# The opening of a two-layer decoder trunk: x, constants, first slabs and first squares in another order

## The reference

```python
for l in range(DEPTH):
    h = rms_norm(x, norm_mix[l])
    q, k, v, hq, hf, hi, hg, cb, cc, ch = split(h @ w_in[l])
    a = sliding window attention with sinks (q, k, v and the cached keys and values)
    o = HGRN2 linear attention (hq, hf, hi, hg), chunked, with a lower bound on the gate
    yc = short convolution of cc * ch
    x = x + concat([a, o, cb * yc]) @ w_out[l]
    h = rms_norm(x, norm_ffn[l])
    gate, up = split(h @ w_gate_up[l])
    x = x + (silu(gate) * up) @ w_down[l]
y = rms_norm(x, norm_final)
```

## Time and profile before

| what | value |
|---|---|
| median of 3 runs | 2764.82 us (2761.4 to 2767.15) |
| span of the profiled execution, first to last instruction | 2763.7 us |
| TensorE busy | 2700.1 us, 98% |
| VectorE busy | 1529.2 us, 55% |
| ScalarE busy | 994.3 us, 36% |
| GpSimd busy | 359.0 us, 13% |
| mean granted clock of TensorE | 0.981 of full |

### The profile page before, as it was taken

The page is one execution under the profiler, slowest core; times in us unless marked ns, Lnnn a source line. Parts: engine busy times, 40 slices in busy tenths (PEclk is TensorE's granted clock), DMA queues, the critical chain, the costliest instruction groups (busy, mean ns, idle before and its releaser), DMA issues.

```text
span 2763.7 us, 53927 instructions
## 1 busy us (share of the span) xinstructions
PE 2700.1 (98%) x19968; PEld 2643.5 (96%) x19968; DVE 1529.2 (55%) x2163; ACT 994.3 (36%) x1322; POOL 359.0 (13%) x343
## 2 busy tenths in 40 slices
PE   6999999999999999999999999999999999999997
PEld 6998899999999999999999898999999999999997
DVE  6465757755554445454544566676555544555555
ACT  3343244433333333333333333344333333333332
POOL 3010101311110001111100011112111100111111
PEclk9999999999999999999999999999999999999998
DMA  6432333454545545444444232335445454454543
GB/s 235 160 116 100 118 123 118 146 173 153 173 161 168 166 152 168 166 160 167 156 164 153 100 131 99 129 125 169 165 157 176 153 175 160 156 169 160 167 169 125
DMA packets 115430, 420.09 MB, mean 152 GB/s; under 512 B 13072, under 2 KB 14352, under 8 KB 115280
## 3 DMA queue, kind: packets, MB, share of 16 engines
q1 hardware_dynamic: 109152, 397.72, 43.1%
q0 software_dynamic: 3168, 14.04, 1.5%
q10 hardware_dynamic: 3024, 7.16, 0.7%
HBM read 411.06 MB, written 11.87 MB: 153 GB/s over the span
## 4 chain that ended last, share of the span: by engine, by line
PE 91%; DVE 4%; issue 2%; ACT 1%; DMA 1%; ACTq 0%; DVEq 0%; POOL 0%; POOLq 0%
PE gp L1343 29%; PE gp L1345 28%; PE gp L1344 27%; PE mb L1396 2%; DVE wlo L628 1%; DVE qp L799 1%; PE mb L1446 1%; PE mb L1412 1%; PE mb L1479 1%; DVE xl L1043 1%; PE mb L1534 0%; PE mb L1491 0%; PE mb L1451 0%; DMA x<-x_in 0%; ACT whi L382 0%
## 5 line engine op out<-in xcount | busy, mean ns | idle before, releaser
L1343 PE MATMUL gp<-xh,whi 128*128 128x288 f32 x4096 | 1239.4, 303 | 29.8 <-DVE wlo L628 27.3
L1344 PE MATMUL gp<-xl,whi 128*128 128x288 f32 x4096 | 1219.2, 298 | 0.0
L1345 PE MATMUL gp<-xh,wlo 128*128 128x288 f32 x4096 | 1215.5, 297 | 0.0
L628 DVE TENSOR_TENSOR wlo<-raw,whi 128x1024 fp32r<-128x1024 f32 x754 | 971.4, 1322 | 369.8 <-ACT whi L382 366.1
L382 ACT ACTIVATE whi<-raw 128x1024 fp32r<-128x1024 f32 x754 | 769.6, 1052 | 622.1 <-PE gp L1345 608.8
L1343 PEld LDWEIGHTS gp<-xh,whi 128*128 128x128 f32 x4096 | 778.7, 190 | 41.8 <-DVE wlo L628 29.3
L1345 PEld LDWEIGHTS gp<-xh,wlo 128*128 128x128 f32 x4096 | 781.6, 191 | 0.0
L1344 PEld LDWEIGHTS gp<-xl,whi 128*128 128x128 f32 x4096 | 780.0, 190 | 1.3
L1343 PE MATMUL gp<-fh,whi 128*128 128x288 f32 x1408 | 416.7, 296 | 0.0
L1344 PE MATMUL gp<-fl,whi 128*128 128x288 f32 x1408 | 415.4, 295 | 0.0
L1345 PE MATMUL gp<-fh,wlo 128*128 128x288 f32 x1408 | 414.0, 294 | 0.0
(11 more groups left out here) (239 smaller groups left out, 2105.0 us busy)
## 6 DMA issues: line engine op xcount, KB each, us to landing
raw<-wstream SPq DMA_DIRECT2D x754, 512.0 KB, 4.0
s<-s_cache POOLq DMA_DIRECT2D x8, 512.0 KB, 4.0
hs_out<-s ACTq DMA_DIRECT2D x8, 512.0 KB, 2.6
caches_out<-caches POOLq DMA_DIRECT2D x1, 3968.0 KB, 15.6
x<-x_in ACTq DMA_DIRECT2D x4, 576.0 KB, 10.4
y_out<-x SPq DMA_DIRECT2D x4, 576.0 KB, 2.8
kct<-kt_cache POOLq DMA_DIRECT2D x4, 512.0 KB, 3.5
vct<-v_cache POOLq DMA_DIRECT2D x4, 512.0 KB, 5.0
```

The source lines that it names most:

```text
L628: v.tensor_tensor(wlo[slot][:], raw[slot][:], whi[slot][:].bitcast(F32), ALU.subtract).then_inc(lo_ready, 1)
L1343: t.matmul(out, w_hi, mv_hi, start=first, stop=False)
L1344: t.matmul(out, w_hi, mv_lo, start=False, stop=False)
L1345: mm = t.matmul(out, w_lo, mv_hi, start=False, stop=last)
```

## The change

Only the order of work changes; what is computed stays the same.

- GpSimd asks for the constants when all four quarters of x have landed. (The copy of the caches stays behind the adds.)
- ScalarE does a one-column copy first, then the exponential of the lower bound, and then, four times, the high part of one slab (0 to 3) and of one quarter of x. VectorE follows in the same order: wlo of a slab, then xl of a quarter.
- The first squares move to ScalarE, behind the last quarter of x, into two buffers in turn (`sq2`, `gs`). GpSimd only adds them. A square from the third on waits for the add before the last.
- The hi and lo of slabs 2 and 3 are out of the first group, and ScalarE's squares take their places between the hi of slabs 4 and on. The first root and its reciprocal come behind the second group, and TensorE does the mean-square products after slab 6 instead of after slab 3.
- So that layer 0 can differ from layer 1, the loop over layers is written out on ScalarE, VectorE, GpSimd and TensorE. TensorE's program has 6186 rows in place of 3241, VectorE's 1192 for 835, ScalarE's 857 for 562, GpSimd's 183 for 166.

```diff
--- before.py
+++ after.py
@@ -273,6 +273,8 @@
         xh_new = sem("xh_new")
         xl_new = sem("xl_new")
         sq_new = sem("square_steps")
+        sq_first = sem("first_squares")
+        sq_added = sem("first_squares_added")
         ms_ready = sem("mean_square_ready")
         root_ready = sem("root_ready")
         rstd_ready = sem("rstd_ready")
@@ -522,11 +524,12 @@
                 a.activation(out[:, 4:8, SEQ:TOK], asb[:], ACT.Copy).then_inc(aa.sem, aa.step("sah"))
                 yield
 
-            def group(n4, s0, m, fills=()):
+            def group(n4, s0, m, fills=(), ready=LEAD):
 
 
                 for s in range(m):
-                    hi(n4, s0 + s + LEAD)
+                    if s + LEAD >= ready:
+                        hi(n4, s0 + s + LEAD)
                     for fill in fills:
                         next(fill, None)
 
@@ -549,23 +552,38 @@
                     pair(i)
 
             a.wait_ge(ones_set, 4)
+            a.activation(one_col[:, 1:2], eps[:], ACT.Copy)
             a.wait_ge(par_loaded, 16)
-            hi(0, 0)
+            a.wait_ge(lb_steps, 2 * DEPTH)
+            a.activation(lbt[:, 2, :], lbt[:, 1, :], ACT.Exp).then_inc(lb_exp, 1)
             for j in range(KC // 2):
+                if j % 2 == 0:
+                    hi(0, j // 2)
                 a.wait_ge(x_loaded[j // 2], 16)
                 for c in range(2 * j, 2 * j + 2):
                     m = a.activation(xh[:, c, :], x[:, c, :], ACT.Copy, scale=par[:, P_AT[P_GAIN] + c:P_AT[P_GAIN] + c + 1])
                 m.then_inc(xh_new, 1)
-                if j == 3:
-                    hi(0, 1)
-            a.wait_ge(lb_steps, 2 * DEPTH)
-            a.activation(lbt[:, 2, :], lbt[:, 1, :], ACT.Exp).then_inc(lb_exp, 1)
-            with a.Fori(0, DEPTH) as l:
+
+            def first_squares():
+
+                for j in range(KC // 2):
+                    if j > 1:
+                        a.wait_ge(sq_added, j - 1)
+                    a.activation((sq2, gs)[j % 2][:], x[:, 2 * j:2 * j + 2, :], ACT.Square).then_inc(sq_first, 1)
+                    if j % 2:
+                        yield
+            for l in range(DEPTH):
                 n4 = l * (SLABS // RING)
                 g = l * GROUPS
-                group(n4, 0, 4)
-                root(l * 2)
-                group(n4, 4, 4)
+                if l == 0:
+                    fill = first_squares()
+                    group(n4, 0, 4, (fill,), ready=4)
+                    group(n4, 4, 4, (fill,))
+                    root(0)
+                else:
+                    group(n4, 0, 4)
+                    root(l * 2)
+                    group(n4, 4, 4)
                 with a.Fori(1, 4) as i:
                     group(n4 + i * 2, 0, 8)
                 a.wait_ge(group_out, hgrn_in(l))
@@ -628,9 +646,10 @@
                 v.tensor_tensor(wlo[slot][:], raw[slot][:], whi[slot][:].bitcast(F32), ALU.subtract
                                 ).then_inc(lo_ready, 1)
 
-            def group(n4, s0, m, fills=()):
+            def group(n4, s0, m, fills=(), ready=LEAD):
                 for s in range(m):
-                    lo(n4, s0 + s + LEAD)
+                    if s + LEAD >= ready:
+                        lo(n4, s0 + s + LEAD)
                     for fill in fills:
                         next(fill, None)
 
@@ -1037,16 +1056,14 @@
             for l in range(DEPTH):
                 lb_step(v.tensor_tensor(lbt[:, 1, l * nh:(l + 1) * nh], lb_col(l), top, ALU.subtract))
             for j in range(KC // 2):
+                if j % 2 == 0:
+                    lo(0, j // 2)
                 v.wait_ge(x_loaded[j // 2], 16)
                 v.wait_ge(xh_new, j + 1)
                 for c in range(2 * j, 2 * j + 2):
                     m = v.scalar_tensor_tensor(xl[:, c, :], x[:, c, :], par[:, P_AT[P_GAIN] + c:P_AT[P_GAIN] + c + 1],
                                                xh[:, c, :].bitcast(F32), ALU.mult, ALU.subtract)
                 m.then_inc(xl_new, 1)
-                if j == 1:
-                    lo(0, 0)
-                if j == 3:
-                    lo(0, 1)
             v.wait_ge(lb_exp, 1)
             lb_step(v.tensor_copy(lbt[:, 0, 0:nh], lbt[:, 2, 0:nh]))
             for l in range(1, DEPTH):
@@ -1061,7 +1078,7 @@
                 lb_step(v.tensor_scalar(oml[:, l * nh:(l + 1) * nh], cur, -1.0, 1.0, ALU.mult, ALU.add))
                 lb_step(v.tensor_scalar(lbc[:, l * nh:(l + 1) * nh], cur, LB_TINY, None, ALU.max))
 
-            with v.Fori(0, DEPTH) as l:
+            for l in range(DEPTH):
                 n4 = l * (SLABS // RING)
                 g = l * GROUPS
                 def in_groups(i):
@@ -1072,7 +1089,15 @@
                         used(n4 + i * 2, 4 * b + 4)
                         out_proj(b, 4 * i + 2 * b)
 
-                in_groups(0)
+                if l == 0:
+                    group(n4, 0, 4, ready=4)
+                    group(n4, 4, 4)
+                    finish_rstd(0)
+                    for b in range(2):
+                        used(n4, 4 * b + 4)
+                        out_proj(b, 2 * b)
+                else:
+                    in_groups(0)
                 with v.Fori(1, 4) as i:
                     in_groups(i)
                 v.wait_ge(const_loaded, 16)
@@ -1261,16 +1286,21 @@
             def sample_rows(sample, T):
                 return sample[bass.ds(T, 1)].rearrange("o p t -> p (o t)")
 
-            e.dma_start(cst[:], consts).then_inc(const_loaded, 16)
-
             squares_start(0)
             e.wait_ge(sq_new, 1)
+            for c in range(4):
+                e.wait_ge(x_loaded[c], 16)
+            e.dma_start(cst[:], consts).then_inc(const_loaded, 16)
             for j in range(KC // 2):
-                e.wait_ge(x_loaded[j // 2], 16)
-                squares(0, j)
+                e.wait_ge(sq_first, j + 1)
+                if j:
+                    e.wait_ge(sq_added, j)
+                e.tensor_tensor(acc2[:], acc2[:], (sq2, gs)[j % 2][:], ALU.add).then_inc(sq_added, 1)
+            e.wait_ge(sq_added, KC // 2)
+            e.sem_inc(sq_new, KC)
 
             e.dma_start(caches_out, caches[:, DEC_SEQ:, :]).then_inc(cache_moved, 16)
-            with e.Fori(0, DEPTH) as l:
+            for l in range(DEPTH):
 
                 e.wait_ge(root_ready, l * 2 + 1)
                 apart(e)
@@ -1562,13 +1592,22 @@
                 yield
 
             t.wait_ge(ones_set, 4)
-            with t.Fori(0, DEPTH) as l:
+            for l in range(DEPTH):
                 n4 = l * (SLABS // RING)
                 g = l * GROUPS
                 xin = from_x(l * 2)
-                group(n4, 0, 4, g, 0, xin)
-                mean_square(l * 2)
-                group(n4, 4, 4, g + 1, 1, xin)
+                if l == 0:
+                    def late():
+                        yield
+                        yield
+                        mean_square(0)
+                        yield
+                    group(n4, 0, 4, g, 0, xin)
+                    group(n4, 4, 4, g + 1, 1, xin, late(), halves=False)
+                else:
+                    group(n4, 0, 4, g, 0, xin)
+                    mean_square(l * 2)
+                    group(n4, 4, 4, g + 1, 1, xin)
                 with t.Fori(1, 4) as i:
                     for b in range(2):
                         group(n4 + i * 2, 4 * b, 4, g + i * 2 + b, b, xin)
```

## The result

The changed kernel takes 2740.68 us (median of 4 runs, 2738.32 to 2745.92) against 2765.99 (4 runs) of the kernel before on the same chip: ratio over the runs 0.9917, 95% interval 0.9898 to 0.9937, so 17 to 28 us faster. The forecast was 2750, the range 2744 to 2760: the sign was right, the time was 9.3 us too long and the range missed it. The profiled execution has a span of 2736.8 us, 26.9 less than before.

The account below looks back on a forecast made before the run. TensorE is busy 98% of the span, so only its holes can be won: 2763.7 - 11.0 (opening) - 4.0 (layer boundary) = 2748.7 profiled, 2750 for the median. Own range 2746 to 2754; 8 in 10 for 2744 to 2760.

Parts of the forecast that it names:

- The twelve small steps: VectorE's lower-bound steps ahead of wlo 4: two get through per GpSimd add, so five adds, 8 us.
- slab 10's load caught: In the opening, slab 10's weight load falls behind the caches' copy, lands at 50.2, and slab 10 starts at 52.6.
- The boundary: Start of layer 1: writing out the layer loop removes a 2.4 us hole and 1.6 of slow pace, 4.0 us.
- (b): Rival: the layer boundary keeps its hole because layer 1's code must be brought in anyway; 2754, chance 0.10.
- (c): Rival: slower, as jumps back in the loop over heads become dear in the longer program; 2774, chance 0.06.
- (d): Rival: no turn-taking to speak of, copy harmless, loads of slabs 8 and 10 in time; 2745, chance 0.12.
- Rival (a): Opening: root waits behind slab 9's caught load, slab 8 starts at 54.5, only 2.5 saved there; 2758, chance 0.24.
- the two small terms of the opening: A 2.8 us hole before slab 4, with wlo 4 ending near 27.5, and 2.1 us of slow pace at slab 10.
- Part 5: Copy against weights in the opening: slab 10 at 52.6 plus 2.1 for slow pace, as good as 54.7 against 65.70.
- The opening: From the start to slab 10: new order of rounding, squares and loads saves 11.0 us.
- Inner loops stay loops, and inside them nothing moves.: Part 6, inside both layers: inner loops are unchanged, and no time gain or loss was counted there.

Follow-up runs that it names:

- e1: The kernel before with only the layer loop written out on four engines, opening unchanged: 2756.66 us, ratio 0.9959 to 0.9983.
- e4: The changed kernel with the first squares back on GpSimd, constants asked for ahead of the last two squares: 2758.01 us, ratio 0.9966 to 0.9991.
- e9: The changed kernel with 15 idle squares on ScalarE ahead of the first rounding: 2763.04 us, ratio 0.9988 to 1.0012.
- e10: The changed kernel with the kernel before's order of rounding, squares left on ScalarE: 2751.65 us, ratio 0.9953 to 0.9983.
- e3: The changed kernel once more, unaltered, for a second profile: 2740.10 us, ratio 0.9894 to 0.9923.
- e2: The changed kernel with each layer in a loop of one trip, so the layer's number is in a register again: 2740.50 us, ratio 0.9903 to 0.9931.
- e5: The changed kernel with VectorE's twelve small lower-bound steps moved behind the first outputs (pj): 2738.66 us, ratio 0.9902 to 0.9929.
- e8: As e6, but the copy of the caches asked for when the first root is done: 2733.26 us, ratio 0.9875 to 0.9907.
- e11: The same kernel as e8 once more: 2734.98 us, ratio 0.9884 to 0.9918.
- e6: As e5, with each whi of slabs 4 to 7 ahead of its two squares on ScalarE: 2737.90 us, ratio 0.9891 to 0.9924.

## Why the prediction missed, step by step

**Right, and shown.** The first product at 9.53 (9.6). Slabs 0 to 3 without a hole, slab 3 ending at 23.8 (24.7). The square on ScalarE 0.67 to 0.69 us (0.7). First add at 17.91 (17.9), last one done at 32.6 (33.4), copy asked for at 33.27 (33.7). The twelve small steps over 7.9 us (8). Slab 8 at 45.37 (44.2), slab 10's load caught, whi at 49.90 (50.2), slab 10 at 52.27 (52.6). The boundary 4.0 (4.0), alone in e1. Rivals (b) and (c) fell with the missing "issue" row, (d) with the waits of 5.16 and 7.61 us. Rival (a) did not come in this kernel (slab 9's load was asked for 1.8 us ahead of the copy), but its mechanism did in e4, e9 and e10, and in e10 nearly its numbers: slab 8 at 55.98 (54.5), slab 10 at 64.21 (63.2). That its margin was thin was right.

**Mis-sized: the two small terms of the opening.** wlo 4 was done near 29, not 27.5, because it shared the turns with the adds itself (four wlo in 8.21 us, 4 x 1.23 alone); hole 5.16, not 2.8. Against that, Part 5 took 2.1 us for a slow pace behind slab 10. The hole there was only 0.25, and slab 10 took 3.30 us. The opening gave 13.3 instead of 11.0: slab 10 started when its load allowed, as forecast, and the slabs ahead of it, late by 1.2 us at slab 8, left it only that small hole.

**The step that failed: "Inner loops stay loops, and inside them nothing moves."** Nothing does move there, and still the heads gave 8.9 us in the profile (6.6 + 2.3). The span was forecast at 2748.7 and came at 2736.8: the 11.9 between them are these 8.9, the opening's 2.3 and 0.7 elsewhere. (The median lies 3.9 above this span, where the forecast had 1.3; hence 9.3 and not 11.9.) The prediction treated a stretch with the same instructions as a stretch with the same time, while the window of the heads already showed a granted clock of 0.95 for 406.7 us: TensorE's pace there was a quantity that could change, and no term or rival held it.

How far do the timed runs bear this out? By the interval of its ratio e3 is 21.3 to 29.3 us below before; opening and boundary are 17.2 of these, so 4.0 to 12.0 are left for the rest. The same sum leaves 0.5 to 8.2 in e2, 0.4 to 7.9 in e5, 1.4 to 8.0 in e9, 0.4 to 7.1 in e1, but -1.8 to 5.2 in e4 and -0.8 to 7.5 in e10. So a gain of several microseconds outside opening and boundary is there; its size of 8.9, and how it differs from kernel to kernel, rest on one profile each.

What the heads' windows show, over all profiles: TensorE is busy for 43.3 to 43.8 us in one at a granted clock of 1.00, and for 46.3 to 48.2 at 0.89 to 0.93, so at the 1.2 GHz level for part of its time. Layer 1's first head took 47.16 us in the kernel before and 43.93 to 43.95 in all twelve profiles with the layers written out (3.2 us). Layer 0's first head took 48.5 to 48.7 us in the three kernels with squares on GpSimd (before, e1, e4) and 43.9 to 47.0 in the ten others (47.04 and 43.95 in the changed kernel's own two). Neither the layer's number in a register (e2) nor the time of arrival (e9) is the cause. **What sends a head to the lower level stays open**; e10, with an opening as long as before's, had the shortest stretch of all (397.7) in its profile, which speaks against the opening's length. That chance alone gave layer 0's heads of before, e1 and e4 their 402.7 to 406.7 against 397.7 to 401.2 in the ten others is unlikely but not excluded, as each has one profile.

## What to carry to other kernels

Behind a long copy the question is which load is asked for just ahead of it, and who stands in line behind the first one that isn't: with slab 8's or 9's load on the other side of the copy, slab 8's wait of 0.4 us became one of 3.9 (e4), 6.0 (e10) or 7.3 (e9), and filling a hole of 5.2 us (e5) brought slab 11 forward by only 1.8, because the next load was caught. Two edits that pass through the same line of waits are priced together, since each alone can be worth nothing. And a forecast lists the stretches whose granted clock is below 1.00 as terms of their own, with a few microseconds of range for each, even where not one instruction moves. One profile of each kernel is too little to tell them apart: two of the same kernel differed by 6.8 us in such a stretch (e8, e11).

## What was not expected of the hardware

The runs of one kernel differ by the granted clock. In the last set the kernel before has 23 runs: the three with a mean clock of 0.979 took 2766.45 to 2769.38 us, the five with 0.983 took 2759.05 to 2760.85, the one with 0.988 took 2749.66. That is 17 to 20 us for 0.009, about 2 us for each 0.001. So the range of 20 us within one kernel is nearly as large as the change's effect, a few runs can stand several microseconds off, and gains of 4 us at slab 11 (e6) are lost in it.

VectorE's short steps share their turns in a regular manner: beside adds of 1.4 to 2.2 us on GpSimd one step of 4 columns is held for 0.99 to 1.41 us until the add ends, and one to three then take 0.06 to 0.18 us each. The held one was in one case a COPY with a single input, 1.41 us. The Trainium skill (SBUF — State Buffer, SBUF: two separate sides) gives the shared ports to whichever starts first, for its whole instruction; the held steps, which end as the add ends, agree.

The copy of the caches went in 80 packets for its 4.06 MB, so some 51 KB each, while the weights' queue moved 435 packets for 1.61 MB beside it (33 to 50 us in the changed kernel), 3.7 KB each. Weight loads asked for 0.6 to 3.7 us behind it took 15.9 to 16.6 us instead of 4.0; the two asked for 1.8 us ahead of it or earlier took 3.3 and 3.4. Whether the size of the packets is the reason was not tested.
